# Products of the modulation rows on GpSimd: a per-partition scalar in place of a broadcast tensor

## The reference

```python
mod = jnp.einsum('bd,de->be', jax.nn.silu(c), w_ada[l]) + b_ada[l]
sh1, sc1, g1, sh2, sc2, g2 = jnp.split(mod[:, None, :], N_MOD, axis=-1)
h = rms_norm(x, norm1_w[l]) * (1 + sc1) + sh1
...
attn = forgetting_attention(qh, kh, vh, log_f)
...
x = x + g1 * (mixed @ w_out[l])
h2 = rms_norm(x, norm2_w[l]) * (1 + sc2) + sh2
x = x + g2 * moe_ffn(h2, ...)
```

## Time and profile before

| | us |
|---|---|
| median of 3 executions | 2324.49 |
| lowest and highest of them | 2315.18 and 2325.43 |
| the profiled execution, whole time | 2321.53 |
| its span, first to last instruction | 2319.9 |
| PE busy in the span | 2186.5 (94%) |
| DVE busy | 1751.8 (76%) |
| ACT busy | 1358.8 (59%) |
| POOL busy | 846.2 (36%), 791 instructions |
| PE's granted clock, mean share of full speed | 0.976 |

### The profile page before, as it was taken

The page is one execution under the profiler, slowest core; times in us unless marked ns, Lnnn a source line. Parts: engine busy times, 40 slices in busy tenths (PEclk is TensorE's granted clock), DMA queues, the critical chain, the costliest instruction groups (busy, mean ns, idle before and its releaser), DMA issues.

```text
span 2319.9 us, 37146 instructions
## 1 busy us (share of the span) xinstructions
PE 2186.5 (94%) x10398; PEld 1807.4 (78%) x10399; DVE 1751.8 (76%) x2141; ACT 1358.8 (59%) x1859; POOL 846.2 (36%) x791
## 2 busy tenths in 40 slices
PE   5999997889966899999999999999999999999997
PEld 4778886776854788888888888888888888888886
DVE  5683423677764799987789977788999779799797
ACT  4332212675224577766667766676777666677675
POOL 2262004884234124443223422232344422244241
PEclk9999998999987999999999999999999999999999
DMA  7234205873336799997779987797999978899795
GB/s 261 89 111 151 60 3 142 243 219 113 106 108 233 237 367 361 388 368 266 261 266 381 376 312 265 232 349 259 390 371 375 342 265 288 300 346 385 260 377 165
DMA packets 298626, 602.85 MB, mean 260 GB/s; under 512 B 24320, under 2 KB 45840, under 8 KB 294928
## 3 DMA queue, kind: packets, MB, share of 16 engines
q1 hardware_dynamic: 270912, 528.95, 63.6%
q0 software_dynamic: 26608, 69.07, 10.8%
q10 hardware_dynamic: 1056, 4.19, 0.5%
HBM read 563.67 MB, written 44.24 MB: 262 GB/s over the span
## 4 chain that ended last, share of the span: by engine, by line
PE 65%; DMA 2%; issue 1%; DVE 0%; POOL 0%; POOLq 0%; DVEq 0%; SPq 0%; ACT 0%; ACTq 0%
PE psum L2227 60%; PE psum L2164 2%; PE psum L2174 2%; PE psum L2209 2%; DMA d_xg<-xn_d,d_entry 1%; DMA d_entry<-list_d 1%; DMA d_bias_rows<-in_b_down_dram 0%; POOL d_spare L1820 0%; DVE d_bhl L2141 0%; POOL d_roww L1879 0%; DVE d_wlo L2049 0%; DVE d_yst L2096 0%; DVEq L1721 0%; DVE d_xtlo L2028 0%; POOLq L1672 0%
## 5 line engine op out<-in xcount | busy, mean ns | idle before, releaser
L2049 DVE TENSOR_TENSOR d_wlo<-d_raw,d_whi 128x1024 fp32r<-128x1024 f32 x578 | 676.3, 1218 | 145.6 <-ACT d_whi L1906 143.7
L1906 ACT ACTIVATE d_whi<-d_raw 128x1024 fp32r<-128x1024 f32 x578 | 579.7, 1054 | 55.3 <-PE psum L2227 50.9
L2227 PE MATMUL psum<-d_whi,d_xthi 128*128 128x512 f32 x1152 | 456.0, 396 | 17.4 <-ACT psum L1964 11.5
L2227 PE MATMUL psum<-d_whi,d_xtlo 128*128 128x512 f32 x1152 | 450.6, 391 | 0.0
L2227 PE MATMUL psum<-d_wlo,d_xthi 128*128 128x512 f32 x1152 | 450.5, 391 | 0.0
L1809 POOL DMA_INDIRECT out_dram<-d_yst,d_dest x49 | 145.8, 2975 | 714.7 <-DVE d_yst L2096 666.7
L2049 DVE TENSOR_TENSOR d_wlo<-slab,d_whi 128x1024 fp32r<-128x1024 f32 x292 | 343.4, 1217 | 21.6 <-ACT d_whi L1906 19.1
L1906 ACT ACTIVATE d_whi<-slab 128x1024 fp32r<-128x1024 f32 x292 | 292.4, 1054 | 6.7 <-PE psum L2227 6.1
L2227 PEld LDWEIGHTS psum<-d_whi,d_xthi 128*128 128x128 f32 x1152 | 217.8, 189 | 63.5 <-issue 13.5
L2227 PEld LDWEIGHTS psum<-d_whi,d_xtlo 128*128 128x128 f32 x1152 | 217.5, 189 | 46.1
L2227 PEld LDWEIGHTS psum<-d_wlo,d_xthi 128*128 128x128 f32 x1152 | 217.7, 189 | 43.6
(11 more groups left out here) (350 smaller groups left out, 4028.1 us busy)
## 6 DMA issues: line engine op xcount, KB each, us to landing
slab<-in_w_gate_up_dram SPq DMA_DIRECT2D x144, 1024.0 KB
d_raw<-in_w_gate_up_dram SPq DMA_DIRECT2D x144, 1024.0 KB
d_raw<-in_w_down_dram SPq DMA_DIRECT2D x144, 1024.0 KB
b_wp<-in_w_ada_dram POOLq DMA_DIRECT2D x16, 1024.0 KB, 9.1
slab<-in_w_in_dram SPq DMA_DIRECT2D x12, 1024.0 KB, 5.3
d_bias_rows<-in_b_gate_up_dram SPq DMA_DIRECT2D x12, 1024.0 KB
d_bias_rows<-in_b_down_dram SPq DMA_DIRECT2D x12, 512.0 KB
a_xin<-in_x_dram ACTq DMA_DIRECT2D x2, 2048.0 KB
```

What stands on the lines that cost most here:

```text
L1906: nc.scalar.activation(whi[n % NW][:, part, :], raw[n % NRAW][:, part, :], ACT.Copy).then_inc(whi_ok, 1)
L2049: nc.vector.tensor_tensor(wlo[n % NW][:, part, :], raw[n % NRAW][:, part, :], whi[n % NW][:, part, :].bitcast(F32), ALU.subtract).then_inc ...
L2227: mm = nc.tensor.matmul(to, m_[:, KH * h + k, :], w_[n % NW][:, k, :], start=(h == 0 and k == 0 and q == 0 and not loaded), stop=(h == 1 a ...
```

## The change

The product of a piece with its per-partition number becomes an instruction with one input tensor and a scalar operand, which is the column `csilu[:, k]`, one number for each partition. The output, the wait in front, the add behind and the transfers stay as they are. 16 instructions are of the new kind.

```diff
                     pool.wait_ge(wp_in[r % 2], 16 * (r // 2 + 1))
-                    own.link(nc.gpsimd.tensor_tensor(wp[r % 2][:, :], wp[r % 2][:, :],
-                                                     s.csilu[:, k:k + 1].broadcast_to([P, PW]), ALU.mult))
+                    own.link(nc.gpsimd.tensor_scalar(wp[r % 2][:, :], wp[r % 2][:, :], s.csilu[:, k:k + 1], None,
+                                                     ALU.mult))
                     own.link(nc.gpsimd.tensor_tensor(s.modacc[:, cols], s.modacc[:, cols], wp[r % 2][:, :], ALU.add))
                     if r + 2 < NPIECE:
                         fetch(r + 2)
```

## The result

The changed kernel takes 2344.29 us (median of 4, 2341.75 to 2346.99) against 2320.50 us of the kernel before on the same chip: ratio 1.0103, 95% interval 1.0083 to 1.0122. It is slower by 23.8 us. The prediction was 2324 with a range of 2314 to 2336 and "no change" at 0.85: wrong. What happened is its rival A, to which it gave 0.13.

The account below looks back on a forecast made before the run. The prediction took the chain PE, ACT, DVE to end the attention stage, with POOL off the path. From 2323 it added 0 for the products and 0.5 + 0.5 for transfers, +1 us: 2324, range 2314 to 2336.

Parts of the forecast that it names:

- rival A: Attention stage: the new product is dearer, and POOL ends the stage from P = 4.3 us a product; chance 0.13.
- What bounds the kernel: End of the attention stage: the chain PE, ACT, DVE arrives last, at 545.81; POOL's speed is not on the path.
- The slack of 3.1 us: End of the attention stage: POOL's last add ends at 542.72, 3.1 us ahead of DVE's last result at 545.81.
- The price of the new product: POOL in attention: P, the time of one new product, taken as 2.1 us against 3.61; effect on the path 0.
- The upper bound of 4.7 us: POOL's new product: at most 0.293 x 2048/128 = 4.7 us, from a cast with nothing counted as fixed.
- The rule cited from the Trainium skill: POOL's new product: one read port, 1.03 cycles an element for one input, an estimate of 1.76 us.
- 477.2 + 16 P: Attention stage: when POOL's list ends, in us, with P the time of one product and no waits for transfers.
- the prediction's check of the formula: POOL's list: P = 3.61 gives 535.0, measured 542.7; the 7.7 between are waits for transfers, 15.2 - 6.8.
- Its starting point, 2323: Whole kernel: 2323 us, the middle of the profiled execution, 2321.5, and the median, 2324.5.
- The transfers: Attention stage: earlier fetches of pieces 2 to 15 delay k tiles, +0.5 us at head 1 and +0.5 at head 3.
- The one-time load: POOL: first call of a freshly loaded routine costs some 6 us; at P = 2.1 hidden by idle time.
- DVE and POOL: Attention stage: the two could hold each other up, but the product meets no such DVE instruction; cost 0.

Follow-up runs that it names:

- the cheap one: The changed kernel with an add of 0.0 as second operation in each of the 16 products: 2321.87 us, ratio 1.0019 to the kernel before.
- the run with all the forms: The kernel before with its 16 GpSimd products written in different forms, one a piece, some cut into smaller instructions; only durations read: 5.45 us for the per-partition scalar alone.

## Why the prediction was wrong

**What bounds the kernel** was right: the stages meet, and the last to arrive sets the time. In all profiles the mixer stage begins 0.33 or 0.34 us behind DVE's last result or 1.83 to 1.84 us behind POOL's last, whichever is later. The slack of 3.1 us overlooked that these two distances differ; it was 1.6. This alone would have lowered the turning point from P = 4.3 to 4.2 us.

**The price of the new product** is the step that failed: "I take 2.1, because reads at one element each about 0.95 ns are what both small rows show". The instruction took 5.45, which for the 16 is 29.5 us more than the old form and 54 more than was assumed. The rows were a cast, a copy and an affine select. What they show is one slope, from 61 ns between two of them; the rows themselves are at 2.3 (293 ns for 128) and 3.6 ns an element (232 for 64). So "every one-input row is near 1 ns an element", the case against rival A, was a reading of that slope and not of the rows. For a copy the slope was right (0.84 ns, 1.90 us at 2048). It was carried over to another routine by likeness, on a name and on the count of inputs. The lone product costs 2.53 ns an element, 5.45 us; the same instruction with a product and an add costs 1.98. The upper bound of 4.7 us, from a 128-column row with nothing counted as fixed, felt wide, but it bounds a cast and not this routine. The trace of before had no row with this routine; the honest bound was open above, with A at more than 0.13.

**The rule cited from the Trainium skill**, "GPSIMD Engine Reference", section 3.1, a body of at most two operations bound by its ports at 1.03 cycles an element, gave the estimate of 1.76 us. The trace agrees for the copy (1.90) and the pair of product and add (1.98), and not for the lone product, which costs three times that. The cost of a one-input instruction does not follow from its port here.

**Rival A** had the mechanism and the arithmetic. Its formula, 477.2 + 16 P, gives 564.4 at P = 5.45; POOL's list ended at 565.0. Over DVE's 545.8 this makes +18.6 us, plus 1.5 for the longer way from POOL to the next stage: 20.1, measured 20.7. That it had all this and still got 0.13 goes back to the price alone. Not all of the dearer price reached the time: 16 x 1.84 = 29.5 us more on POOL's instructions made its list 22.3 us longer, mainly since its waits for transfers shrank by 8.1 us, and the stage's end moved by 20.7. Of the 23.8 us between the medians some 3 are not in the stage's end of the two profiles: 1.3 lie in the stages behind it, and the rest is within the scatter of the executions, which for the kernel before is 10 us. In the prediction's check of the formula the waits are 15.2 - 6.8 = 8.4 us, not the 7.7 that were missing, which changes nothing. Its starting point, 2323, was 2.5 us above the median of four.

**The transfers.** With a dearer product the fetches came later, not earlier, and PE's waits for k tiles fell from 6.4 to 5.4 us. With the cheap one they rose to 7.6: +1.2, where +1 had been counted. The agreement is partly luck: kernels with the dear product had 4.9 to 8.7 us of them. **The one-time load** did not show: the first product took 5.46 us, like the others, and began 0.2 us later than before, as the stage did by 0.3. There it could have hidden in the wait for the first transfer; in the run with all the forms, where the first instruction of this kind was the second piece, it began at 400.25, 0.04 us behind the end of the fetch before it. **DVE and POOL** did not disturb each other, as said: 5437 to 5458 ns for all 16.

## What to carry to other kernels

An instruction that the trace doesn't have must not be priced by its count of inputs; until one row of its own routine is there, the price is open above, and the question to ask is how much dearer it may be before its engine becomes the last one (here, by the formula, 4.2 - 3.6 = 0.6 us an instruction). Work beside the path on an engine that is busy for most of a stage may have next to no slack, so that a dearer form soon costs time (here 20.7 of the 29.5 us that it added), while a cheaper one is worth nothing until something uses the time: here, transfers that step aside for others. And an arrival at a meeting of engines is to be compared with the way from each engine to the next stage added.

## What the runs showed of the hardware

On GpSimd, at 128x2048 in float32, an instruction of one tensor and scalars took 1.91 to 2.05 us for product-add, product-product and add-product, 5.36 to 5.46 for a lone product or add and for a product with an explicit bypass, and 7.16 to 7.19 for add-add, product-maximum and product-subtract. An add of 0.0 behind a product thus made it 2.7 times faster. A product of two full tensors took 4.53 us, and with one repeated column 3.61. At the end of the attention stage it was 0.33 us to the first instruction of the next stage where DVE came last, and 1.84 where GpSimd did.
